# Four reorderings in a hybrid linear-attention layer: held-back input sums, earlier squares, a norm taken apart, a residual in token halves

## What is computed

```python
h = modulate(rms_norm(x), shift1, scale1)
proj = h @ w_in        # gq, gk, gv, g_lr, g_gate, hq, hf, hi, h_gate
forget = lb + (1.0 - lb) * jax.nn.sigmoid(hf)
o_hgrn = chunk_gated_linear_attention(
    silu(hq), 1.0 - forget, hi, log(forget), CHUNK)    # 4 heads, chunks of 64
o_hgrn = merge_heads(rms_norm(o_hgrn, hgrn_norm_g)) * silu(h_gate)
...
x = x + gate1 * (concatenate([o_gla, o_hgrn], -1) @ w_out)
h = modulate(rms_norm(x), shift2, scale2)
x = x + gate2 * (square(relu(h @ w_mlp1)) @ w_mlp2)
return rms_norm(x, final_norm_g)
```

## Time and profile before

| | us |
|---|---|
| median of 3 runs (lowest to highest) | 1164.97 (1164.85 to 1165.19) |
| the profiled execution, its own time | 1166.44 |
| its span, from first to last recorded instruction | 1164.7 |
| PE busy | 1137.4 (98%) |
| PEld busy | 939.3 (81%) |
| DVE busy | 876.3 (75%) |
| ACT busy | 612.9 (53%) |
| POOL busy | 499.4 (43%) |

### The profile page before, as it was taken

The page is one execution under the profiler, slowest core; times in us unless marked ns, Lnnn a source line. Parts: engine busy times, 40 slices in busy tenths (PEclk is TensorE's granted clock), DMA queues, the critical chain, the costliest instruction groups (busy, mean ns, idle before and its releaser), DMA issues.

```text
span 1164.7 us, 15675 instructions
## 1 busy us (share of the span) xinstructions
PE 1137.4 (98%) x5555; PEld 939.3 (81%) x5555; DVE 876.3 (75%) x1048; ACT 612.9 (53%) x933; POOL 499.4 (43%) x318
## 2 busy tenths in 40 slices
PE   7999999899999999999999999999999999999996
PEld 6788788787878787888888888888888888788885
DVE  6898888877777677477976765677795884966776
ACT  7763564756566566345654555455664433424424
POOL 1021111534243344427534353344466675666741
PEclk9999999999999999999999999999999999999999
DMA  9777353044353549421455344544624637447203
GB/s 359 259 235 271 128 175 97 1 127 129 93 177 98 154 123 295 143 93 73 137 170 181 136 155 135 181 144 157 194 64 159 223 91 264 147 132 279 72 1 145
DMA packets 160549, 180.44 MB, mean 155 GB/s; under 512 B 7508, under 2 KB 119256, under 8 KB 157784
## 3 DMA queue, kind: packets, MB, share of 16 engines
q1 hardware_dynamic: 160472, 179.44, 46.4%
HBM read 138.51 MB, written 40.89 MB: 154 GB/s over the span
## 4 chain that ended last, share of the span: by engine, by line
PE 89%; DVE 4%; DMA 2%; ACT 2%; issue 1%; SPq 1%; POOL 1%; DVEq 0%; ACTq 0%
PE unit_bank L1742 16%; PE unit_bank L2156 9%; PE unit_bank L2158 9%; PE unit_bank L2157 9%; PE small_bank L2156 9%; PE small_bank L2158 9%; PE small_bank L2157 9%; PE unit_bank L2003 3%; PE small_bank L1742 3%; PE unit_bank L2005 3%; PE unit_bank L2004 3%; PE small_bank L1879 2%; DVE ada_acc L2257 1%; PE small_bank L1781 1%; DMA ada_slot<-in_w_ada_dram 1%
## 5 line engine op out<-in xcount | busy, mean ns | idle before, releaser
L997 POOL TENSOR_TENSOR wr_lo<-quarter,wr_hi 128x512 fp32r<-128x512 f32 x122 | 197.6, 1632 | 174.4 <-ACT wr_hi L1530 174.3
L2156 PE MATMUL unit_bank<-op_hi,wr_hi 128*128 128x512 f32 x452 | 176.5, 390 | 1.1 <-issue 1.1
L2158 PE MATMUL unit_bank<-op_hi,wr_lo 128*128 128x512 f32 x452 | 175.9, 389 | 0.0
L2157 PE MATMUL unit_bank<-op_lo,wr_hi 128*128 128x512 f32 x452 | 175.9, 389 | 0.0
L2156 PE MATMUL small_bank<-op_hi,wr_hi 128*128 128x512 f32 x448 | 174.5, 390 | 0.0
L2158 PE MATMUL small_bank<-op_hi,wr_lo 128*128 128x512 f32 x448 | 174.3, 389 | 0.0
L2157 PE MATMUL small_bank<-op_lo,wr_hi 128*128 128x512 f32 x448 | 174.3, 389 | 0.0
L1530 ACT ACTIVATE wr_hi<-wr_full 128x512 fp32r<-128x512 f32 x90 | 56.8, 631 | 173.3 <-DVE wr_full L2903 173.3
L2903 DVE TENSOR_TENSOR wr_full<-quarter,quarter 128x512 f32<-128x512 f32 x90 | 88.9, 989 | 56.3 <-PE small_bank L2158 23.0
L1530 ACT ACTIVATE wr_hi<-quarter 128x512 fp32r<-128x512 f32 x136 | 83.0, 626 | 90.5 <-PE unit_bank L2158 48.4
L1742 PE MATMUL unit_bank<-a_hi,w_hi 128*128 128x512 f32 x304 | 121.2, 399 | 0.8 <-DVE w_lo L2401 0.8
(11 more groups left out here) (366 smaller groups left out, 2397.2 us busy)
## 6 DMA issues: line engine op xcount, KB each, us to landing
quarter<-in_w_mlp_dram SPq DMA_DIRECT2D x128, 256.0 KB, 4.1
hidden_scratch<-hid SPq DMA_DIRECT2D x98, 256.0 KB, 2.4
ada_slot<-in_w_ada_dram SPq DMA_DIRECT2D x48, 512.0 KB, 6.1
op_full<-hidden_scratch SPq DMA_DIRECT2D x21, 1024.0 KB, 4.8
pair_quarter<-in_w_in_dram SPq DMA_DIRECT2D x32, 256.0 KB, 3.7
piece_x<-t_scratch SPq DMA_DIRECT2D x16, 512.0 KB, 4.1
piece_y<-t_scratch SPq DMA_DIRECT2D x32, 256.0 KB, 3.3
raw<-in_w_out_dram SPq DMA_DIRECT2D x16, 512.0 KB, 4.5
```

What stands on the lines that cost most here:

```text
L997: pool.tensor_tensor(wr_lo[slot][:, :, :], split_source(n), wr_hi[slot][:, :, :].bitcast(F32), ALU.subtract).then_inc(wr_lo_pool, 1)
L2156: pe.matmul(dst, wh, ah, start=opens, stop=False, skip_group_check=True)
L2157: pe.matmul(dst, wh, al, start=False, stop=False, skip_group_check=True)
L2158: mm = pe.matmul(dst, wl, ah, start=False, stop=k == KH - 1, skip_group_check=True)
```

## The change

Six moves; no arithmetic is added or removed.

- Pieces: piece_x, like piece_y, is loaded by two DMAs of one part each instead of one of both, and TensorE's waits count 32 instead of 16.
- Residual: load_x_back takes one token half at a time; the order of issues becomes x first half of tiles 0 to 3, raw 2, x first half of tiles 4 to 7, raw 3, then the two second halves.
- Squares: on ACT the rounding of the squares comes before the copy of the output bank; it is the order for both halves of each stage.
- Stage's end on ACT: the norm's exponential and P2's high part go behind the tanh of "12"; P7's high part goes ahead of the logarithm. On DVE S2 goes behind the join of "21", and the norm's multiplication behind the gate.
- H0 on DVE: S2 goes ahead of decay and q_cum, and the addition and subtraction for P4's input wait until GpSimd has made P2's low part of the first pair.
- Low squares of the second half: on DVE ahead of the factor of q_rel and S4.

```diff
@@ load_piece
-                if j % 2:
-                    for i in range(2):
-                        sp.dma_start(piece_y[i][:, :].bitcast(F32), t3_dram[:, j, i, :]).then_inc(piece_y_loaded, 16)
-                else:
-                    sp.dma_start(piece_x[120 if p < 5 else 96][:, :, :].bitcast(F32), t3_dram[:, j]).then_inc(piece_x_loaded, 16)
+                for i, part in enumerate(piece_place(p, j)):
+                    sp.dma_start(part.bitcast(F32), t3_dram[:, j, i, :]).then_inc(piece_y_loaded if j % 2 else piece_x_loaded, 16)
...
-            def load_x_back(i):
+            def load_x_back(i, half):
                 sp.wait_ge(six_done, six_of(PAIRS - 1, P4 if i else P5))
-                for half in range(2):
-                    part = slice(half * HALF, (half + 1) * HALF)
-                    sp.dma_start(xT[:, 4 * i:4 * i + 4, part], x_dram[:, 4 * i:4 * i + 4, part]).then_inc(x_back[i][half], 16)
+                part = slice(half * HALF, (half + 1) * HALF)
+                sp.dma_start(xT[:, 4 * i:4 * i + 4, part], x_dram[:, 4 * i:4 * i + 4, part]).then_inc(x_back[i][half], 16)
...
             load_out(1)
-            for i in range(2):
-                load_x_back(i)
-            for v in range(2, 4):
-                load_out(v)
+            load_x_back(0, 0)
+            load_out(2)
+            load_x_back(1, 0)
+            load_out(3)
+            load_x_back(0, 1)
+            load_x_back(1, 1)
...
@@ ACT: output
-                    act.activation(tok(mixed[:, gi + 1], half), src, ACT.Copy).then_inc(read["o"], 1)
                     act.wait_ge(o_squared, before("o", gi) + half + 1)
                     act.activation(sq_hi[:, 0, :], stat[:, 0, :], ACT.Copy).then_inc(sq_hi_ready, 1)
+                    act.activation(tok(mixed[:, gi + 1], half), src, ACT.Copy).then_inc(read["o"], 1)
...
@@ ACT: paired
                 value_of(1, late, "22")
+                pair_high(late + 1, P7)
                 norm_log(1)
-                norm_exp(1)
-                pair_high(late + 1, P7)
-                pair_high(late + 1, P2)
                 value_of(0, late, "21")
                 tanh_of(t0, 1, late, "12")
+                pair_high(late + 1, P2)
+                norm_exp(1)
...
@@ DVE: group
                 read_out(6)
+                if own == "H":
+                    weight_sum_of(0, "S2")
...
                 if own == "H":
-                    weight_sum_of(0, "S2")
+                    dve.wait_ge(pair_lo, PAIR_LO_0 + split_of(0, P2))
                     add_parts(xs[2], 1, 0, 7)
                     subtract(xs[2], xs[2], xs[3], 8)
...
@@ DVE: paired
                 dve.scalar_tensor_tensor(own_cum[:, :], q_rel[:, :], 0.5, own_cum[:, :], ALU.mult, ALU.mult).then_inc(q_cum_ready, 1)
+                low_squares(1)
                 dve.wait_ge(e_q, gi + 1)
                 dve.wait_ge(q_cum_ready, gi + 1)
                 dve.scalar_tensor_tensor(q_rel[:, :], q_rel[:, :], 0.5, t0[:, :], ALU.mult, ALU.mult).then_inc(q_rel_ready, 1)
                 weight_sum_of(late, "S4")
-                low_squares(1)
...
                 weight_sum_of(late + 1, "S3")
+                join(late, "21")
                 weight_sum_of(late + 1, "S2")
-                join(late, "21")
-                norms(1)
                 join(late, "12")
                 silu_of(t0, 1, late, "12", made + 4)
                 gate_half(tok(t0, 1), h, 1, ("12", late + 1))
+                norms(1)
```

More of the change, by code:

```diff
@@ L2019, in seventh_piece @@
                 else:
-                    pe.wait_ge(piece_x_loaded, PIECE_X_0 + 32 * p + 16 * (j // 2 + 1))
+                    pe.wait_ge(piece_x_loaded, PIECE_X_0 + 64 * p + 32 * (j // 2 + 1))
                 wh, wl = pw_hi[place][:, j, :], pw_lo[place][:, j, :]
```

## The result

The changed kernel takes 1171.32 us (median of 5 runs, 1169.22 to 1172.68), the kernel before 1165.19 in the same comparison (5 runs, 1164.85 to 1167.68). The ratio is 1.0045, 95% interval 1.0031 to 1.0059: slower by 5.2 us by the ratio, while the medians lie 6.1 apart. The forecast was slower, by 2.4; the median lies 1.0 us above the top of the wider range, 1170.3. The profiled execution took 1171.32 us, with a span of 1169.6, 4.9 more than the span of before.

The account below looks back on a forecast made before the run. TensorE works nearly all the span, so only its waits can be won. Terms +1.0 - 1.65 + 1.35 + 1.7 = +2.4 on 1164.97 gave 1167.4 us; range 1166.0 to 1169.0, wider 1162.3 to 1170.3.

Parts of the forecast that it names:

- Part 1: End of H0: two pw_lo waits merge into one for k_nat, low clock falls on P6; +1.0 us.
- the row at 360: Profile row: DVE, started 0.05 us ahead of GpSimd, stretched to 1.88; by it H0's term would be +2.1.
- Parts 2 and 5: Squares' rounding ahead of ACT's copy, 0; x pieces in two issues, 0, at most 0.4 us once.
- Part 3: Second-half low squares earlier on DVE: three 0.9 us waits go, stage's end not set by them; S4 0.5 later.
- Part 4: Ends of three paired stages: exponential and P2's high part behind the tanh, tanh 0.55 us earlier each; -1.65.
- Part 6: Residual loads, out projection: unit 2 gains 0.9; dry queue makes unit 4 wait 2.25, start 1.35 later; low clock +1.7.
- Rival (a): Out projection: the clock doesn't fall at unit 4; +0.7, 1165.7 us; chance 0.20.
- (b): Out projection: raw 4 is in time and unit 2's gain stays; -1.55, 1163.4 us; chance 0.15.
- (c): H0's clock recovers at once, stage ends give 1.3 each, raw 4 in time; -5.6, 1159.4; 0.15 together with (e).
- (d): GpSimd gets the port first in H0, 6 us of low clock at unit 4; +4.8, 1169.8 us; chance 0.10.
- (e): Squares' move also helps in half 0 of the paired stages: -0.5 three times; chance 0.15 together with (c).

Follow-up runs that it names:

- pieces alone: The kernel before with piece_x loaded in two issues and nothing else; ratio to the kernel before 0.9995 (0.9986 to 1.0004).
- the squares alone: The kernel before with only the second half's low squares moved ahead of q_rel's factor and S4; ratio to the kernel before 1.0017 (1.0006 to 1.0028).
- The order alone: The kernel before with only the new order of the residual's loads; ratio to the kernel before 1.0025 (1.0011 to 1.0040).
- the halves early: The changed kernel with the two late token halves of x issued ahead of raw 3; ratio to the kernel before 1.0008 (0.9996 to 1.0021).
- the second profile: The changed kernel run once more, unchanged; median 1169.67 us of 8 runs against 1165.91, ratio 1.0037 (1.0025 to 1.0049).

## Why the prediction was wrong in size and right in sign

The sum was +2.4 and the spans differ by 4.9. Every sign that the prediction named came (the waits, the clock behind them, the hole in the DMA share), so the owners of the big waits were right; two terms had the wrong size, for a step left out in each. Term by term, in the profiled pair:

- **Part 1 (H0), +1.0 forecast, +1.5 found.** The mechanism is the forecast one: waits put together, k_nat as the new owner, P6 in the low clock. The updates won 0.86 instead of 1.1, and the clock stayed low for 5.7 us of work behind the restart, inside the 5.2 to 6.0 that the rows of before gave. What the sum left out: the updates run in the low clock too (2.01 to P6's start instead of 1.39), so P6 started 0.24 earlier, not 0.8, although its low part was there in time. Which engine gets the port first came out as taken: q_cum kept its 1.2, and GpSimd's low part beside it took 2.30 instead of 1.29. The Trainium skill (SBUF — State Buffer, Who interferes with whom) lets whoever issues first hold the ports. This trace agrees, with q_cum 0.07 ahead; the row at 360 that the prediction sets against the rule, with a lead of 0.05, stays unexplained. Against the median the term is larger still: the profile of before had an H0 that was 1.1 to 1.2 longer than in four other kernels with the same H0, and against those the four traces with the changed H0 (+0.5 to +1.5) are 1.6 to 2.7 longer, about 2. I had taken the one execution for the typical one.
- **Parts 2 and 5, 0 forecast, 0 found** (the early waits are 0.32, 0.32 and 0.27 us, before 0.32, 0.40 and 0.27; pieces alone 0.9995).
- **Part 3, no gain at the stage's end and 0.5 later per stage by S4 (priced in part 4), found nearly so**: the squares alone make each stage 0.3 to 0.5 longer.
- **Part 4, -1.65 forecast, -0.4 found. This is the step that failed.** The first stage is entered 2.79 later than in the trace of before, and its tanh starts 2.12 later (287.67 against 285.55): 0.67 won, about as forecast (0.55), and the first piece with it. But I followed the exponential and P2's high part only to their own readers, P2's product and the norm. On ACT they had been put in front of the next stage's first instructions, the two copies to v_nat; TensorE's transposes wait for the copies, and 0.52 of the 0.67 went back there. The run with the exponential behind v_nat gets 1.2 of it back and, at -1.6, gives what the sum had said.
- **Part 6, +3.05 forecast, +3.3 found**: -1.0 at unit 2 (-0.9), a wait of 2.36 at unit 4 (2.25), raw 4 issued and landed as the bytes said, and 1.7 for the clock behind it (1.7). The order alone and the halves early show that it is this order and the dry queue. Rival (a), no fall of the clock at unit 4, happens too: among eight traces of kernels with this order and waits of 2.1 to 2.9 the clock fell in five and not in three.
- **Not in the sum: the start**, 1.3 of the 4.9, which differs from execution to execution, as the second profile (3.8) and the squares alone show. Nothing in the one trace of before shows it, and it is bad luck for the first number: the second median, 1169.67, 3.8 above its kernel before, lies inside the range. The MLP and the last us give back 0.8.

The other rivals: (b), raw 4 in time, is out by the wait of 2.36; (c), the stages give all, by that, by the -0.4 and by the low clock behind the 4.62. (d) asked for GpSimd first in H0, which did not happen, though its time, 1169.8, is nearest to the second median. (e) is out by the early waits, which stayed.

What stays open is what makes the clock fall in one execution and not in the next behind nearly the same wait; no run separated it.

## What to carry to other kernels

An instruction that is moved behind something on an in-order engine stands in front of whatever comes next there, in the next stage too: price it for the queue's next customer, not only for its own reader. When a list of waits looks like a list of gains, look for the engine whose unbroken run ends last before TensorE's next step (here ACT's), since here the waits ahead of it only traded places. A load that is put behind another in an issue queue takes over its wait; ask what the transfer queue does meanwhile. And where one execution's clock can be low or not in a stretch, read several before a difference of 1 us is built on one.

## What was not expected of the hardware

- Executions differ by up to 4.1 us before 200, where all these kernels have the same code: from -0.2 to +3.8 over fourteen traces, and the four longest are those with a clock of 0.50 from 45.6 or 46.2 on.
- The load of ACT's function tables took 1.28 us, and the tanh began 0.02 us after it (286.37 + 1.28 against 287.67). The Trainium skill (ScalarE: Activation LUTs, What ACT_TABLE_LOAD costs) adds a drain of about 1.38 us for each switch; as an estimate from that figure the tanh would have come 1.4 us later. No such time stands in this trace, and the measurement decides.
